# Putting the first expert's first half of gate and up between two chunks of the token gather

## The chip, the cores and the metric

The kernel runs on one core of one Trainium2 chip. The metric is the time of one execution on the device in microseconds (us). The times below are medians of several runs of the same program, and the profile comes from one execution.

## The reference, cut to what matters

The model is a first block of two hybrid layers (pooling, short convolution and attention, then a dense feed-forward part), and a second block of two layers whose feed-forward part is a mixture of 16 experts. The change lies in the experts alone, which run once in each of the two layers of the second block:

```python
def grouped_moe(h, router_w, router_bias, w_gate, w_up, w_down):
    ...                       # 256 tokens; each picks 2 of 16 experts, both in one group of 4
    y = jnp.zeros_like(h)
    for e in range(N_EXPERTS):
        a = jax.nn.silu(h @ w_gate[e]) * (h @ w_up[e])     # 1024 -> 512
        y = y + dense_gates[:, e:e + 1] * (a @ w_down[e])  # 512 -> 1024
    return y
```

All numbers are float32. One expert has 6 MB of weights, the 16 of a layer have 96 MB.

## The kernel before, in words

The five engines run programs of their own, written out by hand and tied by semaphores; there is no scheduler, so the order of the source lines of one engine is the order on that engine.

**Tokens.** After the router, each expert gets at most 64 tokens (CAP = 64; a flag turns to `every_expert` when one has more, which does not happen here). A 0/1 matrix `pick` (built by VectorE on line 2067, for 8 experts at a time) gathers them with matmuls: `gather(group, c, bank)` on line 2594 makes chunk c (128 of the 1024 features) of the tokens of 8 experts, 512 columns, in one PSUM bank, with four matmuls (two tiles of tokens, each with the high and the low part of h). KD = 8 chunks make a group. For the first group VectorE copies the even chunks to SBUF (line 2086, semaphore `xg_dve`) and ScalarE the odd ones (line 1171, semaphore `xg_act`). The second group's chunks are gathered one at a time in the course of the first eight experts (`next_group`, line 2666).

**Banks.** The chunks of the first group go to `first_banks` (line 664): bank_xg, bank_tr, bank_y, bank_gu, bank_xg, bank_tr, bank_y, bank_xg for chunks 0 to 7. Only chunk 3 uses bank_gu, the bank in which `gate_up` sums. From chunk 4 on, a gather waits until the earlier user of its bank is copied out (lines 2675 to 2678).

**Experts.** `gate_up(e, half)` (line 2620, matmuls on line 2615) multiplies the 64 tokens of expert e by one half of the rows of its gate and up matrices: 4 chunks, side by side in the array, 16 matmuls of 512 columns. Half 0 needs chunks 0 to 3 and weight units 0 and 1 of the expert, half 1 needs chunks 4 to 7 and units 2 and 3. `tokens_ready` (line 2658) waits for the copies of those chunks for the first expert. After half 1, ScalarE takes silu of the gate (line 1160), VectorE multiplies by up (line 2093), TensorE turns the result (`turn_gathered`), multiplies by the down matrix (`down`, line 2634, units 4 and 5), and adds it back to the tokens' rows (`scatter`, line 2655).

**Weights.** SyncE's queue issues every weight load (line 735), one unit of 1 MB each, into a ring of 24 slots (`raw`, `raw_more`, `raw_deep`), in a fixed order: units 0 to 3 of expert 0, units 0 to 3 of expert 1, units 4 and 5 of expert 0, and so on. The first 24 units of a layer are loaded before its experts begin. Each later one waits until its slot was read: the last matmul of TensorE on a unit raises that slot's `read` semaphore. So the first two loads of the stream wait for `gate_up(0, 0)`, the next two for `gate_up(0, 1)`, the next two for `gate_up(1, 0)`.

**Order around the change**, in `gathered_experts` of TensorE (line 2672): eight gathers, then both halves of `gate_up` of expert 0, then the first chunk of the second group, then the loop over experts 1 to 15.

Of the kernel before, what the change touches and what calls it, by code (L numbers as in the profile page):

```python
# [247 lines left out]
def program(nc, A, out):  # L248
    with ExitStack() as top:
# [1916 lines left out]
        def _(pe):  # L2166
# [245 lines left out]
            for l in range(LAYERS):  # L2412
# [181 lines left out]
                def gather(group, c, bank):  # L2594

                    if c == 0:
                        pe.wait_ge(*pick_ready.at2(l, NT * (group + 1)))
                    for t in range(NT):
                        for h in (h_hi, h_lo):
                            mm = pe.matmul(bank, h[:, t, P * c:P * (c + 1)], pick[:, t, :],  # L2600
                                           start=t == 0 and h is h_hi, stop=t == 1 and h is h_lo)
                    mm.then_inc(gathered.sem, 1)

                def side_by_side(e, i, a, chunk0, column0, order, bank, first, last):


                    units = []
                    for n in range(2):
                        part, there, read, before = ring2(unit_at(e, i + n))
                        pe.wait_ge(*there.at2(l, 16 * (before + 1)))  # L2610
                        units.append((parts_of(part, 4, COLS), read))
                    for c in range(4):
                        for n, (w, read) in enumerate(units):
                            columns = slice(CAP * order[n], CAP * (order[n] + 1))
                            mm = pe.matmul(bank[columns, :], a[:, chunk0 + c, column0:column0 + CAP], w[:, c, :],  # L2615
                                           start=first and c == 0, stop=last and c == 3)
                            if c == 3:
                                mm.then_inc(read.sem, 1)

                def gate_up(e, half):  # L2620

                    side_by_side(e, 2 * half, xg[e // GROUP], 4 * half, CAP * (e % GROUP), (1, 0), bank_gu, half == 0, half == 1)

                def down(e):

                    pe.wait_ge(*ag_ready.at2(l, e + 1))
                    for i in range(4, 6):
                        part, there, read, before = ring2(unit_at(e, i))
                        pe.wait_ge(*there.at2(l, 16 * (before + 1)))
                        w = parts_of(part, 2, D)  # L2630
                        for c in range(2):
                            chunk = 2 * (i - 4) + c
                            for n in range(2):
                                mm = pe.matmul(bank_y[CAP * n:CAP * (n + 1), :], ag[:, CAP * chunk:CAP * (chunk + 1)], w[:, c, COLS * n:COLS * (n + 1)],  # L2634
                                               start=chunk == 0, stop=chunk == 3)
                        mm.then_inc(read.sem, 1)

                def turn_gathered(e):

                    pe.wait_ge(*ax_ready.at2(l, e + 1))  # L2640
                    pe.wait_ge(*place_ready.at2(l, e + 1))
                    for t in range(NT):
                        pe.transpose(bank_tr[:, T + P * t:T + P * (t + 1)], place[:, t, :], ident[:, :])
                    for c in range(4):
                        mm = pe.transpose(bank_tr[:, CAP * c:CAP * (c + 1)], ax[:, P * c:P * (c + 1)], ident[0:CAP, 0:CAP])  # L2645
                    mm.then_inc(ax_turned.sem, 1)

                def scatter(e):

                    pe.wait_ge(*yx_ready.at2(l, e + 1))  # L2650
                    pe.wait_ge(*back_ready.at2(l, e + 1))
                    for t in range(NT):
                        for half in range(2):
                            rows = slice(CAP * half, CAP * (half + 1))
                            mm = pe.matmul(mp[:, 2 * t + half, :], back[rows, P * t:P * (t + 1)], yx[rows, :], start=e == 0, stop=e == NE - 1)  # L2655
                    return mm

                def tokens_ready(e, half):

                    if e == 0:  # L2660
                        pe.wait_ge(*xg_act.at2(l, 2 * half + 2))
                        pe.wait_ge(*xg_dve.at2(l, 2 * half + 2))
                    if e == GROUP:
                        pe.wait_ge(*xg_dve.at2(l, 4 * half + 8))

                def next_group(e):

                    if e < KD:
                        pe.wait_ge(*xg_dve.at2(l, KD // 2 + e))
                        gather(1, e, bank_xg)  # L2670

                def gathered_experts():
                    pe.wait_ge(*hl_ready.at2(l, NT))
                    for c in range(KD):
                        if c >= 4:
                            before = first_banks[:c].index(first_banks[c]) if c < 7 else 4
                            taken = xg_act if before % 2 else xg_dve
                            pe.wait_ge(*taken.at2(l, before // 2 + 1))
                        gather(0, c, first_banks[c])
                    for half in range(2):  # L2680
                        tokens_ready(0, half)
                        gate_up(0, half)
                    next_group(0)
                    for e in range(1, NE):
                        tokens_ready(e, 0)

                        pe.wait_ge(*ax_ready.at2(l, e))
                        gate_up(e, 0)
                        if e >= 2:
                            scatter(e - 2)  # L2690
                        turn_gathered(e - 1)
                        tokens_ready(e, 1)
                        gate_up(e, 1)
                        next_group(e)
                        down(e - 1)
                    scatter(NE - 2)
                    turn_gathered(NE - 1)
                    down(NE - 1)
                    scatter(NE - 1).then_inc(y_done.sem, 1)

                    for c in (gu_done, ab2_turned, down_done):
                        pe.sem_inc(c.sem, NE)
# [45 lines left out]
                with pe.If(dense == 0):  # L2748
                    gathered_experts()
# [26 lines left out]
```

## Time and profile before

| | |
|---|---|
| median of 3 runs | 1762.4 us (1761.14 to 1770.11) |
| profiled execution: first to last instruction | 1763.0 us |
| TensorE matmul busy | 1579.6 us (90%) |
| VectorE busy | 938.6 us (53%) |
| ScalarE busy | 619.9 us (35%) |
| DMA | 427.65 MB, 243 GB/s over the span |
| granted TensorE clock, mean of the span | 0.940 of full speed |

The profiled execution's span is 0.6 us above the median of the runs. How to read the rows further down: a timeline row gives start, length, engine, line, operation, output and inputs, and in brackets how long the engine sat idle before it and what released it. PE is TensorE, DVE is VectorE, ACT is ScalarE, SPq is SyncE's queue of DMA issues. Matmuls overlap, so their starts show the pace, not their lengths.

### The profile page before, as it was taken

Reading aid. Unit: us, or ns where it says so; the run is one execution under the profiler, and the core shown is the slowest. Engines: PE = TensorE matmul, PEld = TensorE weight load, DVE = VectorE, ACT = ScalarE, POOL = GpSimd, SP = SyncE. Lnnn points to the kernel's source line nnn. Section 1 sums busy time; section 2 is a strip of 40 time slices with the busy share of each in tenths; the row PEclk is TensorE's granted clock in tenths of the full one; section 3 lists DMA queues with packets and bytes.
Section 4 is the critical chain, followed back from the end, with each engine's and each line's share of the span. In section 5 each row is a group of like instructions: output and inputs, shape, how many; then the busy total and the mean of one; then the engine's idle time right before and its main releaser. Section 6 shows DMA issues by size and latency. Waiting matters only on the chain.

```text
span 1763.0 us, 18871 instructions
## 1 busy us (share of the span) xinstructions
PE 1579.6 (90%) x7463; PEld 1084.8 (62%) x7463; DVE 938.6 (53%) x1410; ACT 619.9 (35%) x883; POOL 49.4 (3%) x66
## 2 busy tenths in 40 slices
PE   2889999999798999999979996999986996999995
PEld 2777877888676787788868773333335875433331
DVE  5897577874578657764566765111006786211102
ACT  2443534433344454443434642111113572111111
POOL 2000000000000000000030200000000010000000
PEclk8899999999899999999989897999998998899997
DMA  9686445975567534565555335999995417599994
GB/s 344 209 281 213 142 162 174 316 246 212 180 227 272 194 120 167 203 212 183 211 135 188 109 120 213 410 409 409 409 359 177 137 49 283 223 409 409 409 409 170
DMA packets 149963, 427.65 MB, mean 243 GB/s; under 512 B 8104, under 2 KB 16544, under 8 KB 149872
## 3 DMA queue, kind: packets, MB, share of 16 engines
q1 hardware_dynamic: 146192, 417.43, 64.4%
q0 software_dynamic: 3456, 8.87, 1.8%
q8 instruction: 64, 1.05, 0.2%
q14 instruction: 27, 0.22, 0.0%
q10 hardware_dynamic: 224, 0.07, 0.0%
HBM read 425.30 MB, written 1.05 MB: 242 GB/s over the span
## 4 chain that ended last, share of the span: by engine, by line
PE 61%; DVE 19%; SPq 7%; DMA 6%; ACT 4%; issue 3%; DVEq 0%; ACTq 0%
PE gp L2212 26%; PE gp L2615 9%; PE gp L2426 8%; SPq L735 6%; DVE wlo L1330 4%; PE gp L2634 4%; PE mp L2655 2%; DVE acc L1240 2%; DMA raw_more<-in_exp_w_up 2%; PE gp L2600 2%; DMA raw<-in_w_in 2%; ACT whi L843 2%; DMA raw_deep<-in_w_ada 1%; PE mp L2483 1%; PE mp L2482 1%
## 5 line engine op out<-in xcount | busy, mean ns | idle before, releaser
L1330 DVE TENSOR_TENSOR wlo<-raw,whi 128x2048 fp32r<-128x2048 f32 (+1 forms) x132 | 289.2, 2194 | 201.4 <-ACT whi L843 199.5
L843 ACT ACTIVATE whi<-raw 128x2048 fp32r<-128x2048 f32 (+1 forms) x132 | 241.7, 1835 | 309.4 <-PE gp L2212 157.9
L2212 PE MATMUL gp<-whi,xt_hi 128*128 128x512 f32 (+1 forms) x800 | 318.3, 398 | 21.7 <-DVE xt_lo L1391 8.4
L2212 PE MATMUL gp<-wlo,xt_hi 128*128 128x512 f32 (+1 forms) x800 | 310.4, 388 | 0.0
L2212 PE MATMUL gp<-whi,xt_lo 128*128 128x512 f32 (+1 forms) x800 | 310.4, 388 | 0.0
L2212 PEld LDWEIGHTS gp<-whi,xt_hi 128*128 128x128 f32 x800 | 154.0, 192 | 64.0 <-issue 13.1
L2212 PEld LDWEIGHTS gp<-whi,xt_lo 128*128 128x128 f32 x800 | 153.7, 192 | 31.0
L2212 PEld LDWEIGHTS gp<-wlo,xt_hi 128*128 128x128 f32 x800 | 154.2, 193 | 29.2 <-issue 1.0
L2079 DVE TENSOR_SCALAR pr<-slots,key,dg 128x128 f32<-128x128 f32 x64 | 19.3, 344 | 262.2 <-PE gp L2645 262.2
L2426 PE MATMUL gp<-whi,xt_hi 128*128 128x512 f32 (+1 forms) x224 | 86.2, 385 | 5.9 <-DVE xt_lo L1780 3.1
L1240 DVE SCALAR_TENSOR_TENSOR acc<-raw,cact,acc 128x1024 f32<-128x1024 f32 x69 | 88.4, 1282 | 1.9 <-DMA raw<-in_w_ada 0.5
L2093 DVE TENSOR_TENSOR pr<-pr,gp 64x512 f32<-64x512 f32 x32 | 21.7, 679 | 123.2 <-ACT pr L1160 123.2
L2426 PE MATMUL gp<-wlo,xt_hi 128*128 128x512 f32 (+1 forms) x224 | 84.8, 378 | 0.0
L2426 PE MATMUL gp<-whi,xt_lo 128*128 128x512 f32 (+1 forms) x224 | 84.6, 378 | 0.0
L1154 ACT ACTIVATE cgc<-gp 128x256 f32<-128x256 f32 x32 | 12.3, 384 | 187.3 <-PE gp L2645 187.3
L1257 DVE TENSOR_TENSOR wlo<-raw,whi 128x2048 fp32r<-128x2048 f32 (+3 forms) x32 | 59.5, 1859 | 33.9 <-ACT whi L1025 32.6
L2212 PE MATMUL gp<-whi,at_hi 128*128 128x512 f32 x176 | 70.5, 401 | 1.3 <-DVE at_lo L1428 1.3
L2212 PE MATMUL gp<-wlo,at_hi 128*128 128x512 f32 x176 | 69.6, 395 | 0.0
L2212 PE MATMUL gp<-whi,at_lo 128*128 128x512 f32 x176 | 69.5, 395 | 0.0
L2634 PE MATMUL gp<-raw_deep,pr 128*64 128x512 f32 x288 | 65.4, 596 | 1.5 <-ACT pr L1155 1.5
L1025 ACT ACTIVATE whi<-raw 128x2048 fp32r<-128x2048 f32 (+3 forms) x36 | 57.5, 1601 | 25.1 <-PE gp L2426 13.5
L2655 PE MATMUL mp<-pr,cgc 64*128 64x512 f32 x256 | 63.6, 615 | 2.8 <-ACT pr L1165 2.8
(402 smaller groups left out, 2359.9 us busy)
## 6 DMA issues: line engine op xcount, KB each, us to landing
raw<-in_w_in SPq DMA_DIRECT2D x60, 1024.0 KB, 5.9
raw<-in_w_ada SPq DMA_DIRECT2D x42, 1024.0 KB, 5.5
raw_deep<-in_exp_w_down SPq DMA_DIRECT2D x36, 1024.0 KB, 16.9
raw_deep<-in_exp_w_gate SPq DMA_DIRECT2D x30, 1024.0 KB, 14.6
raw_deep<-in_exp_w_up SPq DMA_DIRECT2D x30, 1024.0 KB, 16.7
raw<-in_w_gate SPq DMA_DIRECT2D x20, 1024.0 KB, 5.1
raw<-in_w_up SPq DMA_DIRECT2D x20, 1024.0 KB, 5.2
raw<-in_w_down SPq DMA_DIRECT2D x20, 1024.0 KB, 5.0
```

The source lines that it names most:

```text
L735: sp.dma_start(parts_of(part, units, cols), src).then_inc(there.sem, 16)
L843: act.activation(slot(whi, s % SPLIT, units, cols), slot(raw, g % RAW, units, cols), ACT.Copy).then_inc(hi_done.sem, 1)
L1025: act.activation(slot(whi, s % SPLIT, units, cols), parts_of(part, units, cols), ACT.Copy).then_inc(hi_done.sem, 1)
L1240: ins = dve.scalar_tensor_tensor(out=a, in0=w[:, k, :], scalar=c, in1=a, op0=ALU.mult, op1=ALU.add)
L1257: dve.tensor_tensor(slot(wlo, s % SPLIT, units, cols), parts_of(part, units, cols), slot(whi, s % SPLIT, units, cols).bitcast(F32), ALU.su ...
L1330: dve.tensor_tensor(slot(wlo, s % SPLIT, units, cols), slot(raw, g % RAW, units, cols), slot(whi, s % SPLIT, units, cols).bitcast(F32), AL ...
L2212: mm = pe.matmul(gp[:, q % 2, t, 0:wide], a[:, chunk, ts], w[:, unit, c0:c0 + wide], start=first and n == 0 and m == 0, stop=last and n == ...
L2426: mm = pe.matmul(gp[:, q % 2, t, 0:cols], a[:, chunk0 + unit, ts], w[:, unit, :], start=first and unit == 0 and m == 0, stop=last and unit ...
L2600: mm = pe.matmul(bank, h[:, t, P * c:P * (c + 1)], pick[:, t, :], start=t == 0 and h is h_hi, stop=t == 1 and h is h_lo)
L2615: mm = pe.matmul(bank[columns, :], a[:, chunk0 + c, column0:column0 + CAP], w[:, c, :], start=first and c == 0, stop=last and c == 3)
L2634: mm = pe.matmul(bank_y[CAP * n:CAP * (n + 1), :], ag[:, CAP * chunk:CAP * (chunk + 1)], w[:, c, COLS * n:COLS * (n + 1)], start=chunk == ...
L2655: mm = pe.matmul(mp[:, 2 * t + half, :], back[rows, P * t:P * (t + 1)], yx[rows, :], start=e == 0, stop=e == NE - 1)
```

## The change

TensorE's program alone is reordered: the first half of the first expert's gate and up now stands behind chunk 3 of the gather (with its wait for the copies of chunks 0 to 3), and the second half behind chunk 7. No instruction is added or taken away; chunks 4 to 7 of the gather move behind the first half. It runs once in each layer of the second block.

```diff
@@ -2677,9 +2677,9 @@
                             taken = xg_act if before % 2 else xg_dve
                             pe.wait_ge(*taken.at2(l, before // 2 + 1))
                         gather(0, c, first_banks[c])
-                    for half in range(2):
-                        tokens_ready(0, half)
-                        gate_up(0, half)
+                        if c % 4 == 3:
+                            tokens_ready(0, c // 4)
+                            gate_up(0, c // 4)
                     next_group(0)
                     for e in range(1, NE):
                         tokens_ready(e, 0)
```

## Rows read from the trace of the kernel before

**Rows 1.** The page, part 2: GB/s moved, in 40 slices of 44 us.
```profile
GB/s 344 209 281 213 142 162 174 316 246 212 180 227 272 194 120 167 203 212 183 211 135 188 109 120 213 410 409 409 409 359 177 137 49 283 223 409 409 409 409 170
```

**Rows 2.** The chain that ended last, by time: start, us, what.
```profile
1082.16 9.53 PE gp L2600 x32
...
1279.93 18.72 DMA raw_more<-in_exp_w_up
...
1702.18 18.42 DMA raw_more<-in_exp_w_up
```

**Rows 3.** Timeline, first layer's gather and first expert.
```profile
1087.57 0.40 PE L2600 MATMUL gp<-pick,h_lo 128*128 128x512 f32 x1
...
1088.00 0.60 ACT L1171 ACTIVATE xg_first<-gp 128x512 f32<-128x512 f32 x1 [1.45 <-PE gp L2600]
...
1091.29 0.40 PE L2600 MATMUL gp<-pick,h_lo 128*128 128x512 f32 x1
...
1091.61 4.08 PE L2615 MATMUL gp<-raw,xg_first 128*64 128x512 f32 x17
...
1091.72 1.29 DVE L2067 TENSOR_TENSOR pick<-slots,key 128x512 fp32r<-128x512 f32 x2 [0.24 <-PE gp L2600]
...
1095.10 0.59 PE L2615 MATMUL gp<-raw_more,xg_first 128*64 128x512 f32 x1
...
1098.11 0.59 PE L2615 MATMUL gp<-raw_more,xg_first 128*64 128x512 f32 x1
1098.63 0.50 PE L2600 MATMUL gp<-pick,h_hi 128*128 128x512 f32 x1
```

**Rows 4.** Timeline of TensorE: a matmul that waits for a ScalarE copy.
```profile
1312.83 1.99 PE L2655 MATMUL mp<-pr,cgc 64*128 64x512 f32 x8 [0.70 <-ACT pr L1165]
```

**Rows 5.** Timeline of SyncE's queue: the first loads of each layer's stream.
```profile
1095.29 0.37 SPq L735 DMA_DIRECT2D raw<-in_exp_w_gate  x1
...
1098.72 0.37 SPq L735 DMA_DIRECT2D raw<-in_exp_w_down  x1
...
1103.88 0.37 SPq L735 DMA_DIRECT2D raw_more<-in_exp_w_gate  x1
...
1517.37 0.37 SPq L735 DMA_DIRECT2D raw<-in_exp_w_gate  x1
...
1520.81 0.37 SPq L735 DMA_DIRECT2D raw<-in_exp_w_down  x1
```

**Rows 6.** Windows: length, PE, PEld, DVE, ACT, POOL busy; last PEclk, DMA share, GB/s.
```profile
1096.00:1098.00 2.00, 2.00 (x12) 0.68 (x10) 0.00 (x0) 0.00 (x0) 0.00 (x0) 1.00 0.74 190
...
1104.00:1106.00 2.00, 2.00 (x14) 0.92 (x14) 0.60 (x2) 0.66 (x2) 0.00 (x0) 1.00 1.03 410
...
1518.00:1520.00 2.00, 2.00 (x12) 0.72 (x10) 0.00 (x0) 0.00 (x0) 0.00 (x0) 1.00 0.60 182
```

**Rows 7.** Timeline of TensorE: where it waits for weights, late in each layer.
```profile
1252.75 3.65 PE L2615 MATMUL gp<-raw_deep,xg_second 128*64 128x512 f32 x16 [0.90 <-DMA raw_deep<-in_exp_w_up]
...
1268.10 3.65 PE L2615 MATMUL gp<-raw_more,xg_second 128*64 128x512 f32 x16 [2.00 <-DMA raw_more<-in_exp_w_up]
...
1283.46 5.35 PE L2615 MATMUL gp<-raw_deep,xg_second 128*64 128x512 f32 x16 [2.01 <-DMA raw_deep<-in_exp_w_up]
...
1674.68 3.65 PE L2615 MATMUL gp<-raw_deep,xg_second 128*64 128x512 f32 x16 [0.73 <-DMA raw_deep<-in_exp_w_up]
...
1690.04 5.35 PE L2615 MATMUL gp<-raw_more,xg_second 128*64 128x512 f32 x16 [2.02 <-DMA raw_more<-in_exp_w_up]
...
1705.38 3.65 PE L2615 MATMUL gp<-raw_deep,xg_second 128*64 128x512 f32 x16 [0.30 <-DMA raw_deep<-in_exp_w_up]
...
1720.74 5.35 PE L2615 MATMUL gp<-raw_more,xg_second 128*64 128x512 f32 x16 [2.02 <-DMA raw_more<-in_exp_w_up]
```

**Rows 8.** Windows, columns as in rows 6: most of the first layer's stream, and a slow stretch.
```profile
1096.00:1268.00 172.00, 168.83 (x782) 59.65 (x778) 20.89 (x45) 22.80 (x49) 0.00 (x0) 1.00 1.02 407
...
1285.00:1287.00 2.00, 2.00 (x6) 0.59 (x4) 0.00 (x0) 0.00 (x0) 0.00 (x0) 0.50 1.02 408
```

## The prediction

> **What bounds the kernel now.** The change touches TensorE's order at one place in each of two layers, so I looked for what ends each of those layers. The page's slices come first: in both expert stages the DMA engines move 409 to 410 GB/s slice after slice [rows 1]. The chain of waits then says that this is what counts. At the end of both stages it runs through the landing of a late unit of the up matrices [rows 2], with nothing of TensorE between the issue of that unit and its landing 18 us later. The windows show 407 GB/s over 172 us from the first load on [rows 8], so the stream has no hole. Since the waits for weights at the end of each layer are real pauses of TensorE (0.90, 2.00 and 2.01 us in the first layer, 0.73, 2.02, 0.30 and 2.02 us in the second) [rows 7], TensorE has room before them, and the stream has none. The stage ends when the stream ends, and the stream begins when the first slot is read again. What the change is worth is therefore how much sooner the stream runs, not how much sooner TensorE does anything.
>
> **The change part by part.**
>
> *Nothing added.* The instructions are the same ones. Their matmul time is the same; what can change is the pauses between them, and when the slots come free. I work it out in the first layer's times.
>
> *The first half moves forward.* The last matmul of chunk 3 starts at 1087.57 and ScalarE starts to copy that chunk at 1088.00, 0.43 us later, for 0.60 us; TensorE follows a ScalarE copy by some 0.05 us: where it waits for one elsewhere, the whole pause is 0.70 us [rows 3, 4]. So gate_up(0, 0) can start at 1088.00 + 0.60 + 0.05 = 1088.65. Before, it started at 1091.61 [rows 3]: it comes 2.96 us sooner. Without that wait it would start 0.32 us behind the gather's last matmul (as 1091.61 stands to 1091.29 [rows 3]), at 1087.89, so **the new pause costs 0.76 us**. Before, the copy of chunk 3 was covered by chunks 4 to 7.
>
> *The first two loads.* They were issued at 1095.29 [rows 5] and will be at 1095.29 - 2.96 = 1092.33.
>
> *Chunks 4 to 7.* The last pair of matmuls of a half starts 3.01 us after the pair that opens it (1095.10 to 1098.11), and a gather follows 0.52 us later (1098.11 to 1098.63) [rows 3]. With 0.05 us for the first pair, which starts slower (1091.61 to 1095.10 is 3.49 for eight pairs, 3.01 for seven), the gather resumes at 1088.65 + 3.06 + 0.52 = 1092.23, and its 16 matmuls follow at 0.2325 us each (sixteen steps from 1087.57 to 1091.29 [rows 3]), the last 3.49 us after the first, at 1095.72. All the banks it needs were copied out long ago.
>
> *The second half.* It now stands right behind chunk 7, whose copy by ScalarE is the same 0.43 + 0.60 + 0.05 us: start at 1096.80. Before, it started at 1095.10 with this copy hidden under the first half [rows 3]. So **TensorE is 1.70 us later** from here on: 0.76 for each of the two pauses and 0.09 for each change between the two kinds of matmul (0.52 against 0.43 in the pace of pairs).
>
> *The third and fourth load.* They were issued at 1098.72 [rows 5] and will be at 1100.42.
>
> *The stream.* In the window from 1096 to 1098 the engines moved 190 GB/s x 2 us = 0.38 MB, at 410 GB/s 0.93 us of work [rows 6], so the stream in effect began at 1097.07, which is 1.78 us after the first issue. A unit is 1.049 MB, 2.56 us. Before: two units, and the third begins at 1097.07 + 5.11 = 1102.18. After: the first two are through at 1092.33 + 1.78 + 5.11 = 1099.22, then the engines idle, and the third begins at 1100.42 + 1.78 = 1102.20. **The third unit moves 0.02 us later: the head start of 2.96 us is given back in full.** In the second layer the issues were at 1517.37 and 1520.81 [rows 5] and the window gives 182 x 2 / 410 = 0.89 us, a start at 1519.11 and a delay of 1.74 us [rows 6]; before, the third began at 1524.22, after, at 1520.81 + 1.70 + 1.74 = 1524.25: 0.03 us later.
>
> *The rest of the stream.* The fifth load goes from 1103.88 [rows 5] to 1105.58; the fourth unit is through at 1107.3, 1.7 us later. That is about what a load needs to get up to speed, so nothing or some 0.1 us is lost there. Later loads have growing room, since the stream takes six units, 15.3 us, for an expert, and TensorE 13.35 (1268.10 to 1283.46, less the wait of 2.01 [rows 7]), with some 1.0 us more where it also gathers a chunk (four steps and the two changes).
>
> *Who else hears of it.* VectorE builds the second group's pick only after chunk 7, so it moves from 1091.72 to 1096.15 and takes 1.29 us; its first reader, the gather at 1098.63 [rows 3], moves to 1100.33, so 2.9 us of cover are left. If that were gone the cost would be part of 1.29 us of TensorE's time, not of the stream's. SyncE's and Pool's queues are passed by nothing: no DMA changes its place, SyncE only waits longer between the second and the third load.
>
> *Where TensorE's 1.70 us go.* In the first layer the waits of 0.90 and 2.00 us take them up (0.90, then 0.80 of 2.00), in the second those of 0.73 and 2.02 (0.73, then 0.97) [rows 7]. The landings behind them, on which the end hangs, stay.
>
> Sum: 0.02 + 0.03 us, and up to 0.1 us a layer at the fifth load: about +0.1 us. On the profiled 1763.0 that is 1763.1; on the median of the runs, 0.6 lower, **1762.5 us**.
>
> **Bounds of the unknown terms.** The two pauses are not in the trace. From below, if they cost nothing (the copies seen sooner than I think), the third load is issued 0.18 us later than before instead of 1.70, and the stream gains 1.5 us a layer, 3.0 in all. From above, each costs a copy of VectorE's length, 0.69 instead of 0.60 us, for 0.2 us a layer. I take 0.76, since the 0.70 us row is the same kind of wait [rows 4].
>
> **The clock.** Three of the four waits of 2.0 us are followed by 5.35 us instead of 3.65 for the same 16 matmuls [rows 7], one of them with a row that shows a granted clock of 0.50, the lower level of 1.2 GHz [rows 8]; TensorE had sat idle for 2.01 us before it. The fall costs 1.70 us, on the path only where it comes right behind the last landing that matters, as at 1720.74 in the second layer. Through the pauses up to 0.90 us before 1268 the clock stood at 1.00 [rows 8], the upper level of 2.4 GHz, so I let the new pauses of 0.76 us cost no clock. The Trainium skill, "TensorE: Matmul & The Clock Gate", section "A second HAM failure mode: psum-queue depth-cycling", speaks against this change: it describes an engine that idles for moments between groups of matmuls, as it cycles through PSUM banks, and loses throughput to a clock that falls and rises. The trace so far does not bear it out for pauses under 1 us.
>
> **The rivals.**
>
> A, *the forecast*: stream unmoved, 1762.5. Chance 0.52.
>
> B, *the end's clock turns*. TensorE arrives later at its waits, so the long ones fall elsewhere: a wait behind a slow group is short (0.30 us at 1705.38 between two of 2.02 [rows 7]), so they alternate. In the second layer the wait at 1690 shrinks to 2.02 - 0.97 = 1.05 us. If the clock then holds, the next is 2.0 us with a fall, and the last 0.3 us without: 1.7 us less, 1760.8. For it: the alternation. Against: the first layer may turn the other way by as much, 1764.2. Chance 0.28 for less, 0.06 for more.
>
> C, *the pauses are cheap and the stream starts sooner*: 1.5 us a layer, 1759.5. For it: ScalarE is idle at both copies. Against: the 0.70 us row. Chance 0.06.
>
> D, *slower: the new pauses cost the clock*. This is what the page's section would do here. Place: TensorE falls to 1.2 GHz behind the pause at 1087.9 or 1096.0; price: 1.70 us more for a group of 16 [rows 7]. It decides as soon as the third load is issued later than 1100.4, since the stream idles there already and every us of delay is one of the stage. One fall a layer gives +3.4, 1765.9; two in both layers +6.8, 1769.3. Chance 0.07.
>
> E, *nothing happens* because the copies or the banks hold the first half back to where it was: the loads would stay at 1095.29, 1762.4. Chance 0.01; it can't be told from A by the time.
>
> **How the numbers follow.** The likeliest is A: 1762.5. The range takes in C together with a turned clock on one side (1762.5 - 3.0 - 1.7 = 1757.8) and D's single falls with one turned clock on the other (1762.5 + 3.4 + 1.7 = 1767.6): 1757.8 to 1767.6. A tenth of the chance, D's worst and a disturbed median (one run of before stood at 1770.11), is left out. About 0.5% is what a measurement of this kernel can tell from no change, 8.8 us. None of the cases reaches it alone; only D in all four places with a turned clock does (8.5), or something I have not seen. So faster 0.02, same 0.94, slower 0.04.
>
> **What would show it.** In the profile after: gate_up(0, 0) some 3.0 us sooner behind the gather's start and ScalarE's copy of chunk 3 as its releaser, with a pause near 0.7 us; a second such pause before the second half; the first load some 3.0 us sooner and the third some 1.7 us later against the gather's start; a hole of the DMA engines of about 3 us between the second and the third unit; the late waits for weights shorter by 1.7 us in sum per layer, save for clock; the same time from the gather's start to the landing of the last up unit. Wrong I would be if the third load is issued more than half a us off 1.7, if the hole is absent, if the clock falls near the pauses, or if the chain of waits no longer ends in that landing.

## The result, and the profile after

The changed kernel is slower by a little: 1769.28 us as the median of 20 runs (1765.24 to 1772.88), against 1766.07 for the kernel before in 20 runs (1761.14 to 1770.11). The ratio is 1.0019, 95% interval 1.001 to 1.0028, that is 3.3 us with 1.8 to 4.9. The median of the three runs that stood ahead of the prediction, 1762.4, was 3.7 us below that of the twenty.

| | before | after |
|---|---|---|
| median of 20 runs | 1766.07 us | 1769.28 us |
| profiled execution, first to last instruction | 1763.0 us | 1767.0 us |
| first load of the stream, from the copy of chunk 3 | 7.29, 7.25 | 4.33, 4.33 |
| third load | 10.72, 10.69 | 12.56, 12.59 |
| landing of the late up unit | 210.64, 210.48 | 211.54, 212.13 |

Here and below, times in a layer are counted from the start of ScalarE's copy of chunk 3 (1088.00 in [rows 3]), first and second layer, because the granted clock rises from 0.50 to 1.00 within the gather ahead of it, earlier in one layer and later in the other: the gather took 5.84 and 6.79 us from the first matmul to that copy in the two layers of before.

The timeline of TensorE after, first layer, which answers to [rows 3]:

```profile
1088.59 0.40 PE L2600 MATMUL gp<-pick,h_lo 128*128 128x512 f32 x1
1089.67 3.65 PE L2615 MATMUL gp<-raw,xg_first 128*64 128x512 f32 x16 [0.69 <-ACT xg_first L1171]
1093.25 0.50 PE L2600 MATMUL gp<-pick,h_hi 128*128 128x512 f32 x1
...
1096.82 0.39 PE L2600 MATMUL gp<-pick,h_lo 128*128 128x512 f32 x1
1097.90 0.64 PE L2615 MATMUL gp<-raw,xg_first 128*64 128x512 f32 x1 [0.69 <-ACT xg_first L1171]
...
1100.96 0.59 PE L2615 MATMUL gp<-raw_more,xg_first 128*64 128x512 f32 x1
1101.48 0.50 PE L2600 MATMUL gp<-pick,h_hi 128*128 128x512 f32 x1
```

The two new pauses are there, 0.69 us each, with ScalarE's copy (line 1171) as what ended them. SyncE's queue, which answers to [rows 5]:

```profile
1093.35 0.37 SPq L735 DMA_DIRECT2D raw<-in_exp_w_gate  x1
1093.76 0.47 SPq L735 DMA_DIRECT2D raw<-in_exp_w_up  x1
1101.58 0.37 SPq L735 DMA_DIRECT2D raw<-in_exp_w_down  x1
1101.99 0.47 SPq L735 DMA_DIRECT2D raw_more<-in_exp_w_down  x1
1106.74 0.37 SPq L735 DMA_DIRECT2D raw_more<-in_exp_w_gate  x1
1107.15 0.48 SPq L735 DMA_DIRECT2D raw_more<-in_exp_w_up  x1
1111.08 0.37 SPq L735 DMA_DIRECT2D raw_deep<-in_exp_w_gate  x1
```

Between the second and the third issue lie 7.8 us, where before there were 3.0. The windows (columns as in [rows 6], GB/s last) show the hole that this makes, and, further on, thin places that I had not forecast:

```profile
1099.50:1100.00 0.50, 0.50 (x4) 0.14 (x2) 0.00 (x0) 0.00 (x0) 0.00 (x0) 1.00 1.11 459
1100.00:1100.50 0.50, 0.50 (x4) 0.14 (x2) 0.00 (x0) 0.00 (x0) 0.00 (x0) 1.00 0.44 156
1100.50:1101.00 0.50, 0.50 (x6) 0.14 (x2) 0.00 (x0) 0.00 (x0) 0.00 (x0) 1.00 0.00 0
...
1102.50:1103.00 0.50, 0.17 (x1) 0.00 (x0) 0.50 (x2) 0.00 (x0) 0.00 (x0) 1.00 1.47 106
...
1103.50:1104.00 0.50, 0.50 (x6) 0.18 (x4) 0.10 (x1) 0.00 (x0) 0.00 (x0) 1.00 0.65 270
...
1108.00:1109.00 1.00, 1.00 (x8) 0.31 (x6) 0.11 (x1) 0.16 (x1) 0.00 (x0) 1.00 1.07 377
1109.00:1110.00 1.00, 1.00 (x6) 0.29 (x4) 0.00 (x0) 0.00 (x0) 0.00 (x0) 1.00 0.99 389
1110.00:1111.00 1.00, 1.00 (x7) 0.16 (x3) 0.00 (x0) 0.00 (x0) 0.00 (x0) 1.00 1.01 377
...
1114.00:1115.00 1.00, 1.00 (x8) 0.31 (x6) 0.00 (x0) 0.00 (x0) 0.00 (x0) 1.00 0.86 332
1115.00:1116.00 1.00, 1.00 (x6) 0.29 (x4) 0.00 (x0) 0.19 (x1) 0.00 (x0) 1.00 1.00 365
```

The kernel before has 401 to 418 GB/s in each microsecond from 1104 to 1116, such as

```profile
1109.00:1110.00 1.00, 1.00 (x6) 0.34 (x6) 1.00 (x2) 0.00 (x0) 0.00 (x0) 1.00 1.04 414
1114.00:1115.00 1.00, 1.00 (x8) 0.40 (x6) 0.00 (x0) 0.00 (x0) 0.00 (x0) 1.00 1.04 414
```

The granted clock (third number from the end) is 1.00, its upper level of 2.4 GHz, through both pauses. The late waits for weights of TensorE after, which answer to [rows 7]:

```profile
1270.00 3.65 PE L2615 MATMUL gp<-raw_more,xg_second 128*64 128x512 f32 x16 [1.99 <-DMA raw_more<-in_exp_w_up]
...
1285.36 3.66 PE L2615 MATMUL gp<-raw_deep,xg_second 128*64 128x512 f32 x16 [2.01 <-DMA raw_deep<-in_exp_w_up]
...
1300.70 3.65 PE L2615 MATMUL gp<-raw_more,xg_second 128*64 128x512 f32 x16 [1.99 <-DMA raw_more<-in_exp_w_up]
...
1694.06 5.35 PE L2615 MATMUL gp<-raw_more,xg_second 128*64 128x512 f32 x16 [2.01 <-DMA raw_more<-in_exp_w_up]
...
1724.75 5.35 PE L2615 MATMUL gp<-raw_more,xg_second 128*64 128x512 f32 x16 [2.01 <-DMA raw_more<-in_exp_w_up]
```

The layers still end in a landing, so TensorE's lateness was taken up and what counts is the stream. Adding up the bytes of half-microsecond windows shows where it loses. A unit is 1.049 MB; the table gives when so many units have been moved, counted from the copy of chunk 3 as before.

| units | before | after | lost |
|---|---|---|---|
| 2.5 | 15.28, 15.25 | 15.71, 15.72 | 0.43, 0.47 |
| 5 | 21.69, 21.64 | 22.24, 22.19 | 0.55, 0.55 |
| 8 | 29.37, 29.33 | 30.34, 30.75 | 0.97, 1.42 |
| 70 | 188.25, 188.23 | 189.13, 189.62 | 0.88, 1.39 |

From the eighth unit to the seventieth all kernels of this study take 158.8 to 159.0 us. All that is lost is lost before the eighth.

The 4.0 us between the two profiled executions are 0.90 before the first gather, 1.02 from it to the first layer's landing, 1.44 from there to the second layer's gather, and 0.64 to its landing. The 0.90 and the 1.44 lie where nothing was changed.

### The profile page after: what moved, and what is told of

The parts are those of the page before. It is cut to its first block, busy times and chain, and to the rows that moved or that the text cites. A ratio compares the mean times of both kernels' runs of the same rounds, so it can differ in the third digit from the quotient of the medians.

```text
span 1767.0 us, 18871 instructions
## 1 busy us (share of the span) xinstructions
PE 1580.1 (89%) x7463; PEld 1085.9 (61%) x7463; DVE 938.7 (53%) x1410; ACT 620.2 (35%) x883; POOL 49.7 (3%) x66
## 4 chain that ended last, share of the span: by engine, by line
PE 62%; DVE 18%; SPq 7%; DMA 6%; ACT 4%; issue 3%; DVEq 0%; ACTq 0%
PE gp L2212 26%; PE gp L2615 9%; PE gp L2426 8%; SPq L735 6%; DVE wlo L1330 4%; PE gp L2634 4%; PE mp L2655 2%; DMA raw_more<-in_exp_w_up 2%; PE gp L2600 2%; DMA raw<-in_w_in 2%; ACT whi L843 2%; DVE acc L1240 2%; DMA raw_deep<-in_w_ada 1%; PE mp L2245 1%; DVE ft L1381 1%
```

## The experiments

Each expectation was on record ahead of its run. Times are medians; ratios are to the kernel before on the same chips, with 95% intervals; where two medians are compared, each is uncertain by some 2 us. "Unit 70" and the landing are read from the one trace of each run, as in the table above.

**The change again.**

> The changed kernel once more, on a chip that it shares with the three kernels below. The stage is read from the first gather matmul of a layer to the landing of the last up unit (before: 216.5 us in the first layer). Theory 1 (the third load sets the stream, and the hole ahead of it plus thin places behind it cost some 0.9 us a layer): 1.7 to 2.5 us slower than before, stage 217.4 to 217.6. Rival 2 (the clock falls more often with TensorE later): the stage is only 0.1 longer, and the rest, 3 us, stands in slow groups of matmuls. Rival 3 (the measured 3.3 us is mostly the luck of the clock's phase): under 1 us slower.

1769.39 us, ratio 1.002 (1.0008 to 1.0033). Loads at 4.33 and 12.56, unit 70 at 189.19 and 189.36, landings at 212.79 and 211.93. From the first gather on that is 219.4 and 217.9 us, more than the 217.4 to 217.6 expected; some 0.8 of the first is its slower gather. The slowdown is real, and a loss is there in the stage.

**Only one pause.**

```diff
-                        if c % 4 == 3:
-                            tokens_ready(0, c // 4)
-                            gate_up(0, c // 4)
+                        if c in (4, 7):
+                            tokens_ready(0, c // 6)
+                            gate_up(0, c // 6)
```

> The first half behind chunk 4 instead of chunk 3, the second behind chunk 7. The copy of chunk 3 is then hidden by chunk 4, so one of the two pauses of 0.7 us is gone: first load about 2.8 us sooner than before, third about 1.1 later (1.84 in the changed kernel). Theory 1: the stage is 0.7 us shorter than the changed kernel's, 216.7, and the time 1.5 us under the changed kernel's. Rival 2: no difference to the changed kernel. Rival 3: none that can be measured.

1767.37 us, ratio 1.0001 (0.9987 to 1.0014). First load at 4.50, third at 11.83, unit 70 at 188.36 and 188.65: 0.7 to 1.0 us a layer less than the changed kernel, about as expected, and 2.0 us less in time. The head start is nearly the same as in the change (0.17 us less), so the gain comes from the third load and those behind it, which all come 0.7 us sooner than in the change.

**No pause.**

```diff
-        first_banks = (bank_xg, bank_tr, bank_y, bank_gu, bank_xg, bank_tr, bank_y, bank_xg)
+        first_banks = (bank_xg, bank_tr, bank_y, mp[:, 0, :], bank_xg, bank_tr, bank_y, bank_xg)
...
                     for c in range(4):
+                        if e == 0:
+                            copied = xg_act if c % 2 else xg_dve
+                            pe.wait_ge(*copied.at2(l, (chunk0 + c) // 2 + 1))
...
-                            tokens_ready(0, c // 4)
                             gate_up(0, c // 4)
```

> The change without both pauses: chunk 3 goes to a bank of its own (mp, bank 0), and TensorE waits for each copied chunk just ahead of the matmuls that read it, so that the first half can begin while chunk 3 is copied. First load 3.7 us sooner than before, third 0.3 later. Theory 1: the third unit starts 1.3 us sooner than before, stage 215.2 to 216.0 by how much the hole costs, time 1 to 3 us under before and 4 to 5 under the changed kernel. Rival 2: under before too, as TensorE is no longer late. If the head start itself does the harm (a stream that stops and starts anew), the stage stays above 216.5.

1766.27 us, ratio 1.0 (0.9991 to 1.0009). The loads stand at 3.57 and 11.08, unit 70 at 187.48 and 187.15, so the stream is 0.8 and 1.1 us ahead of before, and 1.6 to 2.5 of the changed kernel. The time is 3 us under the changed kernel's, less than the 4 to 5 forecast, and not under before's.

> The kernel without both pauses once more (chunk 3 in a bank of its own, each copied chunk waited for just ahead of its matmuls), since its time, 1.0000 of before with 0.9991 to 1.0009, leaves its sign open. The stream says unit 70 at 187.2 to 187.5 behind the copy of chunk 3, against 188.24 before, so 0.8 to 1.1 us a layer: 1.7 to 2.1 us under before, and 4 to 5 under the changed kernel. If the stream's end does not carry over to the time: no difference to before again.

Again no gain over before: 1766.47 us, ratio 1.0005 (0.9993 to 1.0018), with unit 70 at 187.15 and 187.99. The four layers seen are 0.25 to 1.1 us ahead in the stream, 0.8 in the mean, and their landings 0.6 ahead of those of the kernels with the order of before. The 1.7 us in all that the stream promises would be a ratio of 0.9990, just outside both intervals; the 1.3 us of the landings, 0.9993, lie within the first interval and at the edge of the second. Whether this version beats the kernel before stays open. A loss is not shown either.

**TensorE late, with no head start.** Matmuls that nothing reads stand between the two halves, in the order of before; first eight, then two:

```diff
                         tokens_ready(0, half)
+                        if half:
+                            for i in range(8):
+                                pe.matmul(mp[:, 0, :], ident[:, :], xg[0][:, i, :], start=True, stop=True)
                         gate_up(0, half)
```

> The order of before, with eight matmuls of 512 columns that nothing reads put between the two halves of the first expert: the first load where it was, the third some 1.8 us later, as in the changed kernel, but with no hole, as the first two units last just until then. Theory 1 with the delay of the third load as the whole cause: the same as the changed kernel, stage 217.3 to 217.6, 1.7 to 2.5 us over before. If the hole and the restart are what costs: stage 216.6 to 216.8, within 0.5 us of before. Rival 2: TensorE is as late as in the changed kernel, so the same time as there, with the stage at 216.6.

1780.09 us, ratio 1.0075 (1.0062 to 1.0088), far over all three numbers, because the dose was wrong: the trace has two records of 0.43 us for each of these matmuls, 16 in 7.13 us at a granted clock of 1.00, which put the third load at 17.94. It still serves. Issued 7.22 us late, with 1.68 us of the first two units left to cover it (10.72 + 1.78 against 14.18), the plain sum says 5.5 us a layer; unit 70 came 6.2 and 6.5 us late. So the sum misses 0.6 to 1.0 us here too, where there is no head start at all.

> The order of before with two matmuls (four passes, about 1.8 us) that nothing reads between the two halves: the first load where it was, the third some 1.8 us later, at 12.5, as in the changed kernel, without a head start and with hardly a hole. If the late third load is the whole cause: unit 70 at 188.4 by the plain sum, at 189.1 to 189.5 if the thin places between the fifth and the eighth unit come with it. If the head start with its hole does the harm, 188.3 and the time of before.

1772.35 us, ratio 1.0031 (1.0018 to 1.0043), third load at 12.75 and 12.79, unit 70 at 189.31 and 189.58, like the changed kernel's. The stream loses as much without a head start; the late third load, and what follows from a late TensorE, is enough for that. The time is 3 us over the changed kernel's, which these two layers of stream don't explain.

**The head start taken away.** SyncE holds the first load until chunk 7 is gathered:

```diff
                     sp.wait_ge(*read.at2(l, before))
+                    if n == S2_MOE + DEEP:
+                        sp.wait_ge(*gathered.at2(l, KD))
```

> The changed kernel, but SyncE holds the first load of the stream until chunk 7 is gathered (the wait would not end in the branch for overfull experts, which these inputs never take). First load 8.2 us behind the copy of chunk 3 instead of 4.33 (before: 7.27), third as in the changed kernel at 12.56. The first two units then last until the third is ready, so there is no hole. If the head start is worth nothing: unit 70 of the stream at 189.1 to 189.5 behind that copy, as in the changed kernel (before: 188.24), and the same time within 1 us. If the hole and the restart are what costs: 188.9, that is only the 0.9 us that the first load is later than before, and some 1 us under the changed kernel. If the head start were worth its 2.96 us: 2 us a layer over the changed kernel.

1773.41 us, ratio 1.0032 (1.0019 to 1.0045). First load at 8.26, third at 12.55, no hole, and yet unit 70 at 189.86 and 190.07: 0.2 to 0.9 us later than the changed kernel, which issues the first load 3.9 us sooner. So 3.9 us of head start buy about 0.6 us of stream. The time is 4 us over the changed kernel's, more than the 1.2 us that the two streams lose; where the rest goes is not shown. Neither the "worth nothing" nor the "hole costs" number was right: without a hole the stream is as thin at the fifth unit (2.88 and 3.16 us for it, 2.56 at the full rate), though its load was issued 2.8 us before four units had been moved.

**The clock out of the way.** Seven matmuls that nothing reads, ahead of `gate_up(e, 0)` of experts 13 to 15, fill TensorE's waits there.

```diff
+                        if e in (13, 14, 15):
+                            for i in range(7):
+                                pe.matmul(bank_xg, h_hi[:, 0, P * i:P * (i + 1)], pick[:, 0, :], start=True, stop=True)
                         pe.wait_ge(*ax_ready.at2(l, e))
                         gate_up(e, 0)
```

> The kernel before, with seven matmuls that nothing reads (1.6 us) ahead of the first half of experts 13, 14 and 15, where TensorE waits 2.0 us for weights. If the falls of the clock behind these waits cost time where they hit the last one: 1.7 us less for each layer whose last wait was followed by a fall, about half of them, so some 1.7 us under before, and no slow group in the last three experts. If the falls cost nothing in the mean: the time of before; if the filler itself ends up on the path: up to 3 us over it.

1766.96 us, ratio 1.0001 (0.9986 to 1.0015): no gain. Its timeline shows that the filler did what it should,

```profile
1718.94 1.88 PE L2689 MATMUL gp<-pick,h_hi 128*128 128x512 f32 x7
1720.99 3.65 PE L2615 MATMUL gp<-raw_more,xg_second 128*64 128x512 f32 x16 [0.17 <-DMA raw_more<-in_exp_w_up]
```

with 3.65 us instead of 5.35 behind the last wait. The 1.7 us expected are just inside the interval, so the cost of the falls in the mean is not settled by it.

> The changed kernel with the same seven matmuls at the same places. With the luck of the clock out of the last experts on both sides, the difference to the run before this one should be what the stream lost: 2.0 to 2.6 us by the streams read so far. If the clock is what made the changed kernel 3.3 us slower: under 1 us.

1767.89 us, ratio 1.0011 (0.9999 to 1.0022), unit 70 at 189.27 and 189.62. By time 0.9 us over the run before it, under the 2.0 to 2.6 expected and on the side of the rival; the errors of the two, about 2 us each, leave both possible. The stream lost as much as in the other traces of the change, and the two landings together come 3.1 us later than those of the run before it, so time and trace don't agree in size here.

**Single loads held, TensorE on time.** The same edit as above in the kernel before, at other loads: the third waits for `ax_ready` 1, the fifth for `ag_ready` 1, the seventh for `xg_dve` of the second group's second chunk.

> The kernel before, where SyncE holds the fifth load until ScalarE has copied the turned result of expert 0 (the wait would not end in the branch for overfull experts): at 17.4 behind the copy of chunk 3 instead of 15.85, with all loads ahead of it unchanged. The fourth unit is through at 19.3, so the lead of the fifth falls from 3.4 to 1.9 us, as in the changed kernel. By the plain sum of the prediction (a load needs 1.78 us to get up to speed) nothing is lost: unit 5 at 21.7, unit 70 at 188.24. If a load needs a longer lead, because the 16 engines do not finish together: unit 5 at 21.9 to 22.1, unit 70 at 188.4 to 188.8.

> The fifth load alone held, once more. By its first trace 0.1 us a layer lost, time 1.0008 of before (0.9987 to 1.0029). Within 1 us of before if single short leads are cheap; 1.5 to 3 us over it if that trace was lucky.

Fifth load at 17.34 instead of 15.85: 1766.3 us (1.0008, 0.9987 to 1.0029) and 1766.42 us (1.0003, 0.9991 to 1.0015). Unit 70 at 188.28, 188.40, 188.49, 188.51: 0.0 to 0.3 us a layer.

> The kernel before, where SyncE holds the third load alone until VectorE has written the first expert's product: at about 12.2 behind the copy of chunk 3 instead of 10.72; TensorE, the first, second, fifth and later loads as before. Lead of the third load over the end of the first two units 2.0 us instead of 3.4. If the losses come one by one from a short lead: unit 2.5 later by 0.1 to 0.4 and nothing behind that, unit 70 at 188.3 to 188.6. If a first thin place makes the later ones dearer, the same here, as the later leads are long.

> The third load alone held, once more and timed. By its first trace it loses 0.1 us a layer at unit 70 (188.31 and 188.36 against 188.24), so within 1 us of before. If the one trace was a lucky draw, as the time of the kernel with the seventh load held suggests (1.0034 of before with a trace that lost nothing): unit 70 at 188.8 or more in one of the layers, and a time 1.5 to 3 us over before.

Third load at 12.2: 1765.1 us in the one run, then 1767.73 us, ratio 1.0013 (0.9999 to 1.0026). Unit 70 at 188.31, 188.36, 188.24, 188.33: 0.0 to 0.1 us. (The four layers with no load held, in the kernel before and in the one with filler, stand between 188.19 and 188.40, so single losses of this size are hardly told from none.)

> The kernel before, where SyncE holds the seventh load until VectorE has copied the second gathered chunk of the second group (same remark on the other branch): at about 22 behind the copy of chunk 3 instead of 20.2. The sixth unit is through at 24.4, so its lead falls from 4.2 to 2.4 us, about that of the changed kernel. Plain sum: unit 8 at 29.35, unit 70 at 188.24. Longer lead needed: unit 8 later by 0.3 to 0.8, unit 70 at 188.5 to 189.0.

> The seventh load alone held, once more: its first trace lost 0.0 to 0.1 us a layer, while its eight timed runs were 4 us over before. If that time was chance: within 1.5 us of before. If the seventh load's lead does cost and the trace was lucky: 2 to 5 us over before, and a thin place between units 6 and 8 in this trace.

Seventh load at 22.3: 1770.41 us (1.0034, 1.0017 to 1.005) and 1769.69 us (1.0024, 1.001 to 1.0037), while unit 70 stands at 188.20, 188.33, 188.49 and 188.36, 0.0 to 0.25 us late. Time and trace disagree here. One of the four landings was late (211.83), the other three were not (210.50, 210.53, 210.69). Slow it is; but for that one landing, to which the last section comes back, the traces that I have don't show where it loses.

**Two and three loads held.**

> As before this one, and the fifth load also held, until ScalarE has copied the turned result of expert 0 (17.35). If each lead counts by itself: the sum of e12 and of e10 (which lost 0.04 and 0.16 us), unit 70 at 188.4 to 188.7. If the second thin place is dearer after a first: a loss of 0.3 to 0.5 us between units 4 and 5, unit 70 at 188.8 or more.

A single run: 1769.36 us. The first layer lost 0.9 us (unit 70 at 189.13), the second 0.2 (188.43).

> The third, fifth and seventh loads held, at about 12.2, 17.35 and 22.3, which is close to the changed kernel's 12.56, 17.72 and 22.07, with TensorE on time and no head start. If the times of the issues alone make the loss, whatever TensorE does: a loss of 0.3 to 0.8 us between units 6 and 7.5 too, unit 70 at 188.9 to 189.4 as in the changed kernel (before: 188.24), time 1.5 to 2.5 us over before. If each lead counts by itself: 188.4 to 188.8. If it takes a late TensorE: 188.3 to 188.5 and the time of before.

```profile
1097.06 0.37 SPq L741 DMA_DIRECT2D raw<-in_exp_w_gate  x1
...
1101.99 0.37 SPq L741 DMA_DIRECT2D raw<-in_exp_w_down  x1
...
1107.15 0.37 SPq L741 DMA_DIRECT2D raw_more<-in_exp_w_gate  x1
...
1112.09 0.37 SPq L741 DMA_DIRECT2D raw_deep<-in_exp_w_gate  x1
```

1770.36 us, ratio 1.0028 (1.0017 to 1.004). Unit 70 at 189.44 and 188.83, 1.2 and 0.6 us late, with the thin place where the changed kernel has it, here the microseconds from 24.0 behind the copy of chunk 3, with the one ahead of them:

```profile
1112.81:1113.81 1.00, 1.00 (x8) 0.42 (x6) 0.00 (x0) 0.00 (x0) 0.00 (x0) 1.00 1.01 401
1113.81:1114.81 1.00, 1.00 (x8) 0.29 (x4) 0.00 (x0) 0.09 (x1) 0.00 (x0) 1.00 0.86 238
1114.81:1115.81 1.00, 1.00 (x8) 0.30 (x6) 0.00 (x0) 0.51 (x1) 0.00 (x0) 1.00 0.88 287
1115.81:1116.81 1.00, 1.00 (x8) 0.42 (x6) 0.00 (x0) 0.00 (x0) 0.00 (x0) 1.00 0.84 340
```

This is most of the changed kernel's loss at unit 70 (0.9 in the mean of two layers, there 1.1 of six), and a time about as far over before, without its order on TensorE, without its pauses and without its head start. The times of the issues are enough, and the single losses (0.1, 0.2 and 0.1 us a layer at unit 70, in the mean) add up to 0.4 and not to the 0.9 of this mean: it takes several short leads in a row, as far as two layers can tell.

## Why the prediction was wrong

*What bounds the stage*: right. In every kernel here the stage ended in the landing, and the stream's 158.8 to 159.0 us from unit 8 to 70 never moved.

*First half 2.96 us sooner*: right, 7.29 to 4.33. *The two pauses*: right, 0.69 us idle and 1.08 from the gather's last matmul to the first of the half, as forecast.

*TensorE 1.70 us later*: 1.84 (third load at 12.56 instead of 10.72). The missing 0.14 are the slow first steps that each change of kind brings: the resumed gather took 3.57 us for its steps, not 3.49, and the second half also opens with a slow pair.

*Third unit 0.02 us later*: mis-sized, measured 0.43 and 0.47 at unit 2.5. 0.14 is the later issue. The rest is that I let the stream of before run at 410 GB/s from its start, while it moved 418 to 422 in its first microseconds, and that a restart took 1.86 us to be worth full rate, not 1.78.

*The rest of the stream, nothing or 0.1 us*: **this is the step that failed.** Between units 2.5 and 8 the changed kernel lost another 0.54 and 0.95 us. I asked only whether a load is issued 1.78 us before the engines run dry. By the bytes moved, the fifth load of the changed kernel comes 1.7 us ahead of the end of the fourth unit (17.72 against 19.45), as forecast, and by unit 5 about 0.1 us is lost, as allowed. The other 0.42 and 0.87 go between units 5 and 8, where I had counted on "growing room". The seventh load does come 2.8 and 3.1 us ahead of the end of the sixth unit, well above 1.78, and still the rate falls to 332 and 365 GB/s in the first layer, after 377 to 389 at the fifth load. In before these leads are 3.2 and 4.0 us, and that of the third load 3.3. Holding the three loads in the kernel before makes most of this loss (1.2 and 0.6 us at unit 70).

Over all traces of this order (six layers, the change, its repeat and the one with filler) the landing is 1.52 us later than in the four layers of the kernels with the order of before (212.16 against 210.64 in the mean, from 210.5 to 210.8 there and 211.5 to 212.8 here). Twice that is 3.0 us, against the 3.3 measured. 2.2 of it is seen at unit 70; the rest is that the landing comes 22.8 us behind unit 70 instead of 22.4, as the parts of a load lie further apart (last section).

*The clock.* The rival that the new pauses cost the clock (D) did not happen: 1.00 in every window near them, in the six layers seen. Its size, 3.4 us for one fall a layer, was right by luck, its mechanism was not. The Trainium skill, "TensorE: Matmul & The Clock Gate", section "A second HAM failure mode: psum-queue depth-cycling", is not borne out by pauses of 0.69 us here. Nor was the clock lower on average: over the whole span it was 0.946 in the twelve runs of the repeat and 0.943 in the runs of before beside them. Rival B, the turn of the late falls, can't be told from chance in these traces: a slow group (5.35 us) behind the last wait is seen in one of two layers of before and in three of four of the changed kernel and its repeat. Each costs up to 1.7 us, so a part of the 3.3 us may be this, as the two runs with filler, only 0.9 us apart, also allow.

*The range.* It ended at 1767.6, 1.7 us short. Of the 6.8 us between forecast and result, 3.7 are the level (three runs of before gave 1762.4, twenty 1766.07) and 3.1 the change. The three runs spread over 9 us, and I treated their median as exact.

*The chance of no change beyond 0.5%* was well placed: the ratio is 1.0019.

## What to carry to other kernels

A stream that bounds a stage is not started sooner by its first load alone: look at the load that comes next after the head start is used up, and at the ones behind it. Loads were free in this kernel while each was issued 3.2 us or more ahead of the moment when all earlier ones had been moved, nearly twice the 1.78 us that a load needs to reach the full rate after an empty queue. One load with 1.6 to 2.0 us cost the stream 0.0 to 0.3 us; several in a row with 1.6 to 3.1 us cost 0.6 to 1.4 us a layer. When an order is changed to free one slot early, list all the issues with their leads, before and after. And take a median of three as no better than its spread.

## What the runs showed of the hardware that I had not expected

A queue that never runs empty can still be thin. In the first layer of the kernel with three loads held, the seventh load was issued 2.8 us before the sixth unit was through, and the engines moved 238 to 340 GB/s for three microseconds instead of 410 [rows 6], at a busy share of 0.84 to 0.88. The loss differs from layer to layer (0.2 and 0.9 us in one run of the same program), and three short leads cost about twice the sum of each alone.

A load does not land at once. The trace keeps sixteen records of landing for each, presumably one for each of the 16 DMA engines, and the load is there with the last. In the kernel before, the sixteen of each of the first four loads lie within 0.4 us of each other; of the load whose landing ends the stage they lie 1.9 and 1.8 us apart, in the six layers of the changed order 1.8 to 3.5, 2.7 in the mean. This spread grows in jumps and mostly stays to the end of the stage. In the layer of the kernel with the seventh load held that landed late (211.83), it jumps from 0.3 to 3.1 us at the seventh load, while unit 70 is only 0.2 us late. Of the 1.5 us by which the landings of the changed order are late, the first of the sixteen records is 0.8 late, and the wider spread makes the other 0.7. That the parts come apart is shown; that an engine ahead of the others runs dry while they still work is then a likely reason for the thin places, but why the parts come apart, and what each waits for, is not shown.

One thing stays open: times and streams do not always agree in size. With only the seventh load held, the timed runs were 4 us over before in two sets, and the traces' streams no more than 0.5 in all; the kernel with two extra matmuls was 3 us slower than the changed one with the same loss in the stream, the one with the head start taken away 4 us slower with 1.2 us more; and the one without pauses gained in the stream and not in time. The loss in the stream is shown; that it is all of the 3.3 us is not.
